# A root that is taken out of the transposes and put in afterwards: scaled copies and a row

## The reference

```
h    = x * rsqrt(mean(x*x) + eps) * g_pre            # per token, per column
proj = h @ w_in                                      # 2048 -> 5952 columns, cut into q, k, v, gates, latents
q, k = rmsnorm and rope of heads; latents rmsnorm'ed; softmax attention in three variants
o    = attention output * silu(gate)
y    = o @ w_out
x    = x + rmsnorm(y) * g_post
```

## Time and profile before

| | us |
|---|---|
| median of 3 executions | 2951.66 (2950.23 to 2952.61) |
| the profiled execution | 2954.75 |
| its span | 2953.1 |
| PE busy | 2896.9 (98%) |
| DVE busy | 2128.6 (72%) |
| ACT busy | 1310.0 (44%) |
| POOL busy | 331.4 (11%) |

### The profile page before, as it was taken

The page is one execution under the profiler, slowest core; times in us unless marked ns, Lnnn a source line. Parts: engine busy times, 40 slices in busy tenths (PEclk is TensorE's granted clock), DMA queues, the critical chain, the costliest instruction groups (busy, mean ns, idle before and its releaser), DMA issues.

```text
span 2953.1 us, 43096 instructions
## 1 busy us (share of the span) xinstructions
PE 2896.9 (98%) x15984; PEld 2476.0 (84%) x15984; DVE 2128.6 (72%) x2851; ACT 1310.0 (44%) x1660; POOL 331.4 (11%) x359
## 2 busy tenths in 40 slices
PE   7999999999999999998999999999999999999998
PEld 6888787888787898987888888888888888877886
DVE  5687777687776857777479688447884488888745
ACT  5343454443543333754356444434444344444443
POOL 1001020011021101020078400000000000000001
PEclk9999999999999999999999999999999999999999
DMA  8867477766567867256545554555545555454553
GB/s 316 295 219 280 164 264 250 277 245 244 191 231 279 295 258 263 93 208 218 187 168 188 186 180 175 188 196 186 183 172 192 192 186 185 170 179 177 187 197 142
DMA packets 99614, 620.62 MB, mean 210 GB/s; under 512 B 11056, under 2 KB 11184, under 8 KB 37040
## 3 DMA queue, kind: packets, MB, share of 16 engines
q1 hardware_dynamic: 70560, 509.88, 48.1%
q0 software_dynamic: 28944, 109.26, 10.4%
HBM read 616.99 MB, written 2.10 MB: 210 GB/s over the span
## 4 chain that ended last, share of the span: by engine, by line
PE 91%; DVE 4%; ACT 2%; DMA 1%; issue 1%; POOL 1%; DVEq 0%; SPq 0%; POOLq 0%; ACTq 0%
PE ps L566 29%; PE ps L1010 17%; PE ps L530 16%; PE ps L576 15%; PE ps L1086 5%; DMA aring<-in_ada 1%; PE ps L972 1%; ACT BIG L1157 1%; DVE wl L1900 1%; PE ps L736 1%; PE ps L775 0%; PE ps L851 0%; PE ps L660 0%; DVE BIG L2367 0%; DVE aring L1916 0%
## 5 line engine op out<-in xcount | busy, mean ns | idle before, releaser
L1157 ACT ACTIVATE wh<-ring 128x2048 fp32r<-128x2048 f32 (+1 forms) x498 | 894.5, 1802 | 1325.0 <-PE ps L576 674.9
L1900 DVE TENSOR_TENSOR wl<-ring,wh 128x2048 fp32r<-128x2048 f32 (+1 forms) x433 | 986.1, 2277 | 582.6 <-ACT wh L1157 321.4
L566 PE MATMUL ps<-hhl,wh 128*128 128x512 f32 x3712 | 898.6, 394 | 4.5 <-DVE hhl L1888 4.5
L566 PEld LDWEIGHTS ps<-hhl,wh 128*128 128x128 f32 x3712 | 683.2, 189 | 139.4 <-issue 6.4
L530 PE MATMUL ps<-wh,hhl 128*128 128x512 f32 (+1 forms) x1728 | 528.4, 386 | 6.4 <-DVE wl L1900 4.2
L576 PEld LDWEIGHTS ps<-hhl,wl 128*128 128x128 f32 x3712 | 477.1, 192 | 18.2
L576 PE MATMUL ps<-hhl,wl 128*128 128x256 f32 x3712 | 482.2, 283 | 0.0
L530 PEld LDWEIGHTS ps<-wh,hhl 128*128 128x128 f32 x1728 | 321.9, 188 | 76.3 <-DVE wl L1900 10.7
L530 PE MATMUL ps<-wl,hhl 128*128 128x512 f32 (+1 forms) x864 | 331.7, 384 | 0.0
L1916 DVE SCALAR_TENSOR_TENSOR aring<-aring,BIG 128x1024 f32<-128x1024 f32 x192 | 233.5, 1221 | 56.9 <-DMA aring<-in_ada 54.9
L1681 POOL DMA_DIRECT2D aring<-in_ada x192 | 102.6, 534 | 873.7 <-DVE aring L1916 859.1
(11 more groups left out here) (307 smaller groups left out, 2477.6 us busy)
## 6 DMA issues: line engine op xcount, KB each, us to landing
ring<-in_stream SPq DMA_DIRECT2D x480, 1024.0 KB, 4.8
aring<-in_ada POOLq DMA_DIRECT2D x192, 512.0 KB, 5.0
BIG<-in_nbr_bias POOLq DMA_DIRECT2D x2, 1024.0 KB, 5.2
BIG<-in_g_post POOLq DMA_DIRECT2D x2, 1024.0 KB, 5.1
out<-X SPq DMA_DIRECT2D x4, 512.0 KB, 2.7
BIG<-in_decays POOLq DMA_DIRECT2D x2, 768.0 KB, 6.3
X<-in_x SPq DMA_DIRECT2D x1, 1024.0 KB, 7.0
X<-in_x SPq DMA_DIRECT2D x2, 512.0 KB, 8.9
```

The source lines that it names most:

```text
L566: mm(ps[:, 4 + c, :], wh[:, c % 2, k * P:(k + 1) * P], hhl[:, k, :, :].rearrange("p a b -> p (a b)"), start=(k == 0), stop=False, skip_gro ...
L1157: return nc.scalar.activation(o, i, func, **kw)
L1900: return tt(blocks(wl[:, c % 2, :], cols), blocks(ring[:, c, :], cols), blocks(wh[:, c % 2, :].bitcast(F32), cols), ALU.subtract)
```

## The change

PE transposes X itself, not Xn. The first two parts are transposed at once, the other two between the first and the second slice. X's blocks are released by DVE's update, without a wait for the root. The root comes back in two ways: the copies of the token-first groups take `rstd2` as a scale (a value per partition, so one instruction per token tile), and feature-first chunks are multiplied by `rrow`, a 128x256 tile that holds the root of each token in every partition. PE makes it with two small products (`root_row`), and DVE copies it out of PSUM. `keep_awake` runs 20 products in the loop and 20 after it. The last norm, in front of the second block, is as before.

```diff
-            def transposed(i, part, banks=T_BANKS):
+            def transposed(i, part, banks=T_BANKS, src=X):
...
-                                                Xn[:, t, k * P:(k + 1) * P], ident)
+                                                src[:, t, k * P:(k + 1) * P], ident)
...
+            def root_row(l):
+
+                pe.wait_ge(prs_done, l + 1)
+                for t in range(T):
+                    last = mm(ps[:, 7, t * P:(t + 1) * P], rstd2[:, t:t + 1].to_broadcast([P, P]), ident, start=True, stop=True)
+                last.then_inc(rrow_full, 1)
+
             pe.wait_ge(small_ready, 16)
+            for j in range(3):
+                pe.wait_ge(x_load[j], 16)
             with pe.Fori(0, LAYERS) as l:
-                for part in range(3):
+                for part in range(2):
                     transposed(l, part)
                 for i in range(TM_G - 2):
-                    rows_group(..., rest=() if i else ((l, 3),))
+                    rows_group(..., rest=() if i else ((l, 2), (l, 3)))
+                root_row(l)
                 for p, cols in ((0, 512), (1, TM_END)):
+                    if p:
+                        pe.wait_ge(rrow_done, l + 1)
...
                     if j == 0:
                         pe.wait_ge(lat_done, 3 * l + 3)
+                        pe.wait_ge(fm_scaled, (l + 1) * FM_C)
...
-                keep_awake(40, 7)
+                keep_awake(20, 7)
+            keep_awake(20, 7)
...
+            def rooted_out(g, col, pair, cols=512):
+                act.wait_ge(unit_done, g * R + R)
+                for t in range(T):
+                    last = f(PT[:, t, col:col + cols], ps[:, 2 * pair + t, 0:cols], ACT.Copy, scale=rstd2[:, t:t + 1])
+                last.then_inc(tm_free, 1)
...
-                rows_out(PT, l * LAYER_G, 0, 0)
+                act.wait_ge(prs_done, l + 1)
+                rooted_out(l * LAYER_G, 0, 0)
...
-                        shape(PF, l * FM_C + (j - 2), j - 2, ACT.Silu)
+                        shape(PF, l * FM_C + (j - 2), j - 2, ACT.Silu, fm_scaled)
...
-                        x_done if block == 3 else xb_done, 1)
+                        xn_done if l + 1 < LAYERS else x_done if block == 3 else xb_done, 1)
...
+            def rooted_sum(n, c, chunk):
+
+                column_sum(PF, n, c, chunk)
+                dve.wait_ge(fm_free, R + n + 1)
+                tt(PF[:, chunk, :], PF[:, chunk, :], rrow, ALU.mult).then_inc(fm_scaled, 1)
...
             take_gains(0)
+            dve.sem_inc(xn_done, 8)
             for l in range(LAYERS):
-                dve.wait_ge(prs_done, l + 1)
-                for block in range(3):
-                    if l:
-                        if block == 2:
-                            x_block(l - 1, block)
-                        next_block(l - 1, block)
-                    else:
-                        normed(block)
...
+                    if l and b in (1, 3):
+                        x_block(l - 1, 2 + b // 2)
...
+                    if j == 1:
+                        dve.wait_ge(rrow_full, l + 1)
+                        v.tensor_copy(rrow, ps[:, 7, 0:SEQ]).then_inc(rrow_done, 1)
...
-                        column_sum(PF, l * FM_C + (j - 1), (j - 1) % R, j - 1)
+                        rooted_sum(l * FM_C + (j - 1), (j - 1) % R, j - 1)
```

More of the change, by code:

```diff
@@ L279, in block @@
         krot = area(0, 2, T, 64)
+        rrow = area(256 + DM, SEQ)
         qkT = area(WH, QK_HEADS, SEQ)
@@ L402, in block @@
         yrs_done = sem("yrs_done")
+        rrow_full, rrow_done, fm_scaled = sem("rrow_full"), sem("rrow_done"), sem("fm_scaled")
         pe_passed, pool_passed, dve_passed = sem("pe_passed"), sem("pool_passed"), sem("dve_passed")
@@ L599, in transposed @@
                             last = pe.transpose(ps[:, banks[b], kk * SEQ + t * P:kk * SEQ + (t + 1) * P],
-                                                Xn[:, t, k * P:(k + 1) * P], ident)
+                                                src[:, t, k * P:(k + 1) * P], ident)
                     last.then_inc(ht_full, 1)
+            def root_row(l):
[3 more added lines that the diff above has]
+                last.then_inc(rrow_full, 1)
             pe.wait_ge(small_ready, 16)
+            for j in range(3):
+                pe.wait_ge(x_load[j], 16)
             with pe.Fori(0, LAYERS) as l:
-                for part in range(3):
+                for part in range(2):
                     transposed(l, part)
                 for i in range(TM_G - 2):
-                    rows_group(l * LAYER_G + i, l * TM_N + i, i % 2, layer=None if i else l, rest=() if i else ((l, 3),))
+                    rows_group(l * LAYER_G + i, l * TM_N + i, i % 2, layer=None if i else l, rest=() if i else ((l, 2), (l, 3)))
+                root_row(l)
                 for p, cols in ((0, 512), (1, TM_END)):
+                    if p:
+                        pe.wait_ge(rrow_done, l + 1)
                     rows_group(l * LAYER_G + (TM_G - 2 + p), l * TM_N + (TM_G - 2 + p), p, cols)
@@ L757, in between_first @@
                 if s < 3:
-                    transposed(LAYERS, s + 1, TM2_BANKS)
+                    transposed(LAYERS, s + 1, TM2_BANKS, Xn)
                 gates(s)
-            transposed(LAYERS, 0, TM2_BANKS)
-            transposed(LAYERS, 1, TM2_BANKS)
+            transposed(LAYERS, 0, TM2_BANKS, Xn)
+            transposed(LAYERS, 1, TM2_BANKS, Xn)
             pe.wait_ge(c2_ready, 16)
@@ L1210, in next_high, with rooted_slots @@
                 high(g + (c + 1) // R, (c + 1) % R, free, cols).then_inc(hi_done, 1)
+            def rooted_slots(g, col, pair, cols=512, after=512):
+                for c in range(R):
+                    next_high(g, c, False, cols if c < R - 1 else after)
+                rooted_out(g, col, pair, cols)
+            def rooted_out(g, col, pair, cols=512):
[3 more added lines that the diff above has]
+                last.then_inc(tm_free, 1)
             def rows_slots(dst, g, col, pair, free=False, cols=512, after=512):
@@ L1224, in half_out, with shape @@
                 f(dst[:, chunk, :], ps[:, 4 + c, SEQ:2 * SEQ], ACT.Copy).then_inc(half_done, 1)
-            def shape(dst, n, chunk, func):
-                act.wait_ge(fm_free, n + (R + 1))
+            def shape(dst, n, chunk, func, summed=None):
+                if summed is None:
+                    act.wait_ge(fm_free, n + (R + 1))
+                else:
+                    act.wait_ge(summed, n + 1)
                 act.sem_inc(act_passed, 1)
@@ L1250, in _ @@
                     next_high(l * LAYER_G, c)
-                rows_out(PT, l * LAYER_G, 0, 0)
+                act.wait_ge(prs_done, l + 1)
+                rooted_out(l * LAYER_G, 0, 0)
                 for i in range(1, TM_G - 2):
-                    rows_slots(PT, l * LAYER_G + i, i * 512, i % 2)
+                    rooted_slots(l * LAYER_G + i, i * 512, i % 2)
                 g = l * LAYER_G + (TM_G - 2)
-                rows_slots(PT, g, (TM_G - 2) * 512, 0, after=TM_END)
-                rows_slots(PT, g + 1, (TM_G - 1) * 512, 1, cols=TM_END)
+                rooted_slots(g, (TM_G - 2) * 512, 0, after=TM_END)
+                rooted_slots(g + 1, (TM_G - 1) * 512, 1, cols=TM_END)
                 for j in range(FM_C - 1):
@@ L1842, in next_block @@
                 else:
-                    dve.wait_ge(xb_done, 6 * l + 2 * (block + 1))
+                    dve.wait_ge(xb_done, 2 * (block + 1))
                 normed(block)
@@ L1953, in _ @@
             dve.sem_inc(a_used, 2)
-            dve.sem_inc(x_done, 2)
+            dve.sem_inc(x_done, 2 * LAYERS)
             def take_gains(l):
@@ L2062, in _ @@
                     if j:
-                        column_sum(PF, l * FM_C + (j - 1), (j - 1) % R, j - 1)
+                        if j == 1:
+                            dve.wait_ge(rrow_done, l + 1)
+                        rooted_sum(l * FM_C + (j - 1), (j - 1) % R, j - 1)
                     if j == 1:
@@ L2092, in _ @@
                         modulation(l_ada + ADA_TM // 2, a)
-                column_sum(PF, l * FM_C + (FM_C - 1), R - 1, FM_C - 1)
+                rooted_sum(l * FM_C + (FM_C - 1), R - 1, FM_C - 1)
                 for b in (1, 3):
```

5 lines of the change are left out of this document (removed).

## The result

The changed kernel takes 2955.84 us in the median of 16 runs (2951.19 to 2958.71), the kernel before 2951.82 in the median of 16. The ratio is 1.0014, 95% interval 1.0008 to 1.0021: slower by 2.4 to 6.2 us. The middle of that, 4.1, is inside the bound of 0.2% (5.9 us), the upper end is just past it. The time is inside the range of the forecast. Its point, 2952.6, was 3.2 us too low, and the time lies at rival 2 (2956.4). The profiled execution took 2957.01 (span 2955.3, 2.2 more than before).

A forecast was written before the change was run, and what follows sets the result against it. PE's largest wait was taken as the bound: transposes 18.4 us behind DVE's normalising. Start -2.05, between layers -3.5, copies +2.7, feature-first +3.8 gave +0.95 on the median 2951.66: 2952.6 us, range 2946.5 to 2957.5.

The forecast's parts named there:

- rival 2: Feature-first units: layer 1 falls into the slow load pattern too, as a late DVE issues loads back to back; +4.75, 2956.4, chance 0.12.
- The start: First transposes no longer wait for root and normalising; slice 3 comes 2.0 us earlier, taken as -2.05, ends -0.6 and -2.8.
- Between the layers: A shorter spin lets transposes start 4.55 us earlier; slice 1 and later come 3.5 us earlier, ends -2.5 and -4.7.
- Token-first copies: Split scaled copies cost PE 0.25 at group changes, `root_row` 0.45 per layer; +2.7 for both layers, ends 1.4 and 3.2.
- Feature-first units of layer 0: Multiplications make DVE late behind slow `aring` loads of 5.4 us; PE 3.0 later, another 0.8 at the end: +3.8.
- 6 x 0.46 = 2.76: DVE's lag in us by the low part of unit 12, from six steps without idle time, 0.46 more each.
- The sum of the later units: Layer 0: 2.76 brought along, some 0.7 won back, 5 x 0.46 more; low part of unit 22 about 3.4 us later.
- a named sign of being wrong: The prediction is wrong if DVE's waits for `aring` shrink instead, or if PE waits elsewhere.
- 4.6 us of room: Unit 12's low part was there at 212.3 and wanted at 216.9, enough room for DVE's 2.76 us lag.
- Feature-first units of layer 1: Loads take 4.2 us, so a double step costs DVE less than PE's 11.1 and it catches up; cost 0.
- The sum: All terms together, -2.05 - 3.5 + 2.7 + 3.8 = +0.95 us against the median before.
- Rival 3: PE's clock is low in a slice 0, at the start or between the layers; +5.95, 2957.6, chance 0.08.

The follow-up runs named there:

- a2: The changed kernel with one plain ScalarE copy per token-first group in place of two with the root as scale; 2953.97 us, ratio 1.0008.
- c1: The changed kernel with the multiplication of chunk 3 moved to step 5, behind the sum of chunk 4, in each layer; 2949.87 us, ratio 1.0001.
- b4: The changed kernel with the multiplication of chunk 3, in step 4, put behind the sums of the heads' squares in each layer; 2955.75 us, ratio 1.0018.
- b3: The changed kernel with the spin as in the kernel before, 40 in the loop of layers and none behind it; 2963.01 us, ratio 1.0038.
- b1: The changed kernel with ScalarE making the next slice's high part first and the two scaled copies after it at each token-first group change; 2952.42 us, ratio 1.0006.
- a3: The kernel before with one more VectorE operation of 128x256 behind each of its 48 feature-first sums, and waits for it; 2958.24 us, ratio 1.0025.
- a1: The changed kernel without the multiplications of the 48 feature-first sums by the row of roots; 2946.73 us, ratio 0.9987.
- c3: The kernel before with four of the eighteen modulations of each feature-first stage done earlier and nothing else; 2952.95 us, ratio 1.0006.
- a4: The changed kernel with the multiplications of the first ten chunks of each layer on GpSimd in place of VectorE; 2952.52 us, ratio 1.0009.

## Why the prediction came out as it did

**The start**, -2.05: right, -2.25 measured, by the chain that was named (two banks, a table load, the Silu, the first modulations, a low part). One reading was wrong. Slice 3 of the kernel before did not wait for its low part: that was there at 38.45, PE came from slice 2 at 38.76, and neither PE nor its weight loads waited for anything between 28 and 44 us. The chain became the limit only in the changed kernel, where slice 3 waits 0.55 us for it. And the lower clock level, which was given 0.9 us of slice 0, took nothing here and up to 2 us in the other traces (17.1 to 19.2 in a2). In the eleven traces with this start the fifth slice begins 1.5 to 2.4 us earlier than the 44.20 of the kernel before (42.70 in c1, 41.78 in b4), so the forecast sits in the middle of what the start gives.

**Between the layers**, -3.5: right, -4.2 measured. The gap between spin and transposes was 1.50 us here instead of 1.87; over all runs it is 1.5 to 2.0, in b3 1.93. Nothing that the traces show fills it, and behind layer 1, where the loop falls through, it is 0.2, so it is still read as the way back to the top of the loop; no run takes the loop away. (The row names VectorE's update of X as the releaser. But the first transposes wait for its first two operations of four, done at 440.79 + 2 x 0.69 = 442.2, so that what is left is the way back.) The other 0.3: the eight transposes that were moved behind slice 0 cost 0.6, not 1.0 (slice 0 to slice 1 takes 7.24 where it took 6.66). The eight that stood there before had waited for VectorE's normalising (a weight load, 0.49 us at 454.59), and now none does.

**Token-first copies**, +2.7: right. In layer 0 the first unit begins 0.88 us earlier and the first group's copy 2.25: 1.4, as forecast. With 1.7 in layer 1 it is 3.1. a2 and b1 show the way that was named, copy, high part, low part. Of it 1.9 are the copies' own 0.2 per change, 0.7 the row's products (0.36 in each layer, 0.45 forecast). Some 0.3 is slice 3 of layer 1: it waits for its low part as slice 3 of the start does (a weight load waits 0.39 us at 464.96), which the forecast did not have. The last 0.2 is not traced to anything.

**Feature-first units of layer 0**, +3.8: near in size, +3.4 measured, and in part by luck.

- The prediction had read the 1.13 us of idle time ahead of the low part of unit 6 as room that covers the added work. It was GpSimd's room, and VectorE waits 2.13 us for the power instead. The lag "6 x 0.46 = 2.76" was 4.75 at the low part of unit 12. Without that wait, in c1, it is 2.78, as forecast.
- The sum of the later units is off: 2.76 - 0.7 + 5 x 0.46 is 4.4, not 3.4. Carried through, the prediction's own terms give +4.8 for the layer.
- On the other side `aring` landed in 5.0 us and not in 5.4, and VectorE's waits for it shrank from 16.8 to 11.4 us. That was a named sign of being wrong; it took up what was too much. The low part of unit 22 was 3.5 us late.
- PE's waits were to come in the last three units. They come in units 12, 19, 20 and 22: at unit 12, where 4.6 us of room had been counted, the low part was ready at 216.19 and PE was there first.

With the wait for the power gone, in c1, this stage costs 2.5 in its one profile.

**Feature-first units of layer 1**, 0: this is the step that failed, "In layer 1 the loads take 4.2 us [...] it catches up, and the cost is 0". The loads took 5.0 and the stage grew by 3.0 us. Rival 2 had the outcome, and its reason is not borne out. A DVE that is late and slow loads together cost PE its waits: a3 shows that the multiplications alone bring them in both layers, a1 that without them PE waits for nothing. But lateness is not what makes the loads slow. From 638 to 708 us the median landing of `aring` is 4.7 to 5.2 us in the traces of all thirteen other kernels, in a1 (4.8) and c3 (4.8) too, which have no multiplications. From 210 to 280 us it is 4.3 to 5.1 in these thirteen, and 5.4 in the kernel before. So the pair of 5.4 and 4.2 is found in one profiled execution only, and 4.2 was no property of layer 1. Whether the kernel before shows it again is open, as only one of its executions was profiled.

**The sum**: -2.25 - 4.2 + 3.1 + 3.4 + 3.0 = +3.05 against +0.95 forecast, +3.2 at the spin behind layer 1. What comes behind it (two slices at a fallen clock, +3.2, less 1.0 in waits, and the 3.5 that come back at 1381) takes 1.3 off in this execution. Rival 3, a slow slice 0 at the start or between the layers, did not come in the changed kernel; part of it is in other traces, 2 us of slice 0 at the lower level at the start (a2) and slow transposes between the layers (a3 and b3, both with the spin of 40). The clock fell behind layer 1 instead, and there in kernels of both kinds.

**What it means for the change.** It wins 6.5 us at two places where PE waits, and gives 9.5 back on engines that had looked idle on average. Leaving out the multiplications is worth 7.9 us, about the most that a better place for them can give. Moving one per layer by one step gives 3.8 by the medians and 1.6 in the stages of the profile; how much of that is the move and how much the fall of the loads is not shown. That the move takes VectorE's wait away is.

## What to carry to other kernels

Idle time ahead of an instruction is not free room until it is known who else uses it: here 1.13 us of VectorE's idle time were the slot of GpSimd's operations, and 0.46 us of work in it cost 2. When a lag on a second engine is worked out, use the slowest landing that any stage of the profile shows, not the one of the stage at hand, unless something is known that fixes it; a second profile of the same kernel would have shown how far a stage's landing can be trusted. And where two engines share the last word in a group change, the order of two instructions on one of them (high part first, copies after) can be worth more than what was added: 0.4 us per change here, where the second copy had added 0.2.

## What the runs showed of the hardware

Operations of GpSimd that fall under a low part of VectorE (128x2048, 2.29 us) are held up, by about what is left of it: three small ones take 2.75 us for 0.75 and end at 177.76, the low part at 177.71; a power takes 6.20 for 4.20 when it begins 0.15 us after the low part (b4). A power that begins 0.03 us ahead of it is not held up, and the low part takes 2.34 (c1). In the other direction a multiplication of 128x256 on GpSimd made VectorE's operation beside it 0.42 us longer (a4). In the changed kernel PE ran its first slice at the upper clock level after 3.7 us of nothing but transposes; in eight of ten other traces with the same start the rise came later, up to 2.1 us into the slice (a2). The gap between the end of PE's loop body and its first product of the next turn was 1.5 to 2.0 us, and 0.2 where the loop falls through. And of fourteen profiled kernels with nearly the same work, the first slice behind layer 1 fell to the lower level in six, before and after the change, with nothing in the edits that goes with it.
